# Where three operands of TensorE lie in the on-chip memory, modulo 512 bytes

## The chip, the cores and the metric

The kernel runs on one core of one Trainium2 chip. The metric is the device time of one execution in microseconds; the median of three runs of the kernel before is 2125.82 us (2125.45 to 2138.95).

## What is computed

Two stacks of transformer-like layers work on one sequence of 256 positions with 1024 channels, all in float32.

```
first stack, 2 layers:
  x -> hybrid_mixer (w_in 1024x7680; differential attention, neighbourhood attention, short
       convolution; gates; w_branch 3x512x1024; w_mix_out 1024x1024) -> layer_norm(alpha*x + h)
    -> memory_cross_attention (xa_q, xa_kv, xa_o) -> layer_norm(alpha*x + h)
    -> conv_ffn: (silu(dwconv(gt) + b) * u) @ w_out, with u, gt = split(x @ w_in), D_FF 2816
       -> layer_norm(alpha*x + h)
second stack, 2 layers:
  x + 0.5*swiglu(rms_norm(x))  ->  x + mix @ w_out  (pool, block attention, dilated attention,
  31-tap convolution; the four branches stand side by side in mix)  ->  x + 0.5*swiglu(rms_norm(x))
swiglu(x) = (silu(x @ wg) * (x @ wu)) @ wd, D_FF 2816
```

Nearly all the arithmetic lies in the products with weights.

## The kernel before, in words

**Weights.** All weight matrices are cut on the host into 336 chunks of 128 x 2048 floats (1 MB). SyncE fetches each into one of five slots of `raw`. ScalarE copies a chunk into one of four slots of `whi` with rounding to the reduced float32 format of TensorE (L782), and VectorE writes what is left, raw minus whi, into `wlo` (L1599). `wlo` and `raw` lie at the same addresses. In the same way each activation is kept in two parts: `xh` and `xl` for x, `fh` and `fl` for the gated product of the feed-forwards, `zh` and `zl` for the four branches of the second stack's mixer, `yh`/`yl`, `mh`/`ml`, `oh`/`ol` and `memh`/`meml` for the branches, the merged branches, the attention's output and the memory of the first stack.

**Products.** `product` (L1192) issues 48 matmuls of a chunk in a row, in 16 groups of three: the upper weights with the upper activation, the upper weights with the lower activation, the lower weights with the upper activation. Each has its own weight load of 128 x 128 floats and streams 256 columns; both operands come from the on-chip memory. All go through the helper `mm`, whose line is L1156, so this line stands for every matmul but the transposes (L1342, L1368, L1395). With kinds F, B and O the weight chunk is the stationary operand and the activation the moving one; with kind T it is the other way round (`va`, `vb`, `xv`, `up`, `vm`, `vd`).

**Order.** `plan` writes the order of all chunks out by hand: in each layer of the first stack the mixer (roles dq, dk, va, qb, kb, vb, gc, hc, gb, gate, branch, mo), the cross attention (xk, xv, xq, xo) and the feed-forward (fu, fg, fo; 33 chunks); in each layer of the second stack a feed-forward (sg, su, sd; 33 chunks), the mixer (cg to vd, then wo) and another feed-forward. Attention steps stand between the chunks as `steps`. TensorE takes everything in this order; at the end of a stage it waits for the norm of x.

**Addresses.** `sb` takes the tiles one behind the other, in the order of the program. A tile of n floats takes 4n bytes of each partition, rounded up to 32. The weights are first: `wlo` at byte 0 and `whi` at 40960, with slots of 8192 bytes and weight tiles of 512 bytes, so every weight tile begins at 0 modulo 512. Then comes `x` (8192 bytes), then `lead`, a tile that nothing uses: 48 floats, 192 bytes. So `xh`, `xl` and each of their 1024-byte rows begin at 192 modulo 512. `trail` (80 floats) fills up to 512 bytes. Further on, `lead_f` puts `fh` and `fl` at 192 modulo 512 and `lead_z` puts `zh` and `zl` at 320. `yh`, `yl`, `mh`, `ml`, `oh`, `ol`, `memh` and `meml` lie at 192 as well. Below, the **offset** of a matmul is the address of its moving operand minus that of its stationary operand, modulo 512.

| matmuls | chunks | offset before | offset after |
|---|---|---|---|
| kind F with xh, xl | dq, dk, qb, kb, gc, hc, gb, gate, xq, fu, fg, sg, su, cg, ca, qm, km, qd, kd | 192 | 128 |
| kind T with xh, xl | va, vb, up, vm, vd | 320 | 384 |
| fh, fl | fo, sd | 192 | 64 |
| zh, zl | wo | 320 | 224 |
| yh, mh, oh, memh as moving operands | branch, mo, xo, xk | 192 | 192 |
| memh, meml as stationary operands | xv | 320 | 320 |

Of the kernel before, what the change touches and what calls it, by code (L numbers as in the profile page):

```python
# [22 lines left out]
P = 128  # L23
# [215 lines left out]
def kernel_program(nc, xT, memT, consts, consts2, pos, par1, par2, bias, W, out):  # L239
# [3 lines left out]
    with ctx:  # L243
        def sb(name, shape, dt=F32, where=ctx):
            return where.enter_context(nc.sbuf_tensor(name, shape, dt))
# [8 lines left out]
        wlo = sb("wlo", [P, RAW_RING, CH], F32R)  # L254
        whi = sb("whi", [P, HI_RING, CH], F32R)
        x = sb("x", [P, KT, S])
        _lead = sb("lead", [P, 48])
        xh = sb("xh", [P, KT, S], F32R)
        xl = sb("xl", [P, KT, S], F32R)
        _trail = sb("trail", [P, 80])  # L260
        c0 = sb("c0", [P, NC0])
        ones = sb("ones", [P, P])
        par = sb("par", [P, NP1])
# [65 lines left out]
        ff = ExitStack()  # L329
# [12 lines left out]
        fa = sb("fa", [P, 512], where=ff)  # L342
        fth = sb("fth", [P, 512], where=ff)
        fp = sb("fp", [P, 512], where=ff)
        _lead_f = sb("lead_f", [P, 120], where=ff)
        fh = sb("fh", [P, 2, 2, S], F32R, ff)
        fl = sb("fl", [P, 2, 2, S], F32R, ff)
        posf = sb("posf", [P, S], where=ff)
        posi = sb("posi", [P, S], mybir.dt.int32, ff)
        hpad = sb("hpad", [P, 2, S + TAPS - 1], where=ff)  # L350
        sgm = sb("sgm", [P, 512], where=ff)
        yc = sb("yc", [P, 2, S], where=ff)
        yc2 = sb("yc2", [P, 2, S], where=ff)
        _lead_z = sb("lead_z", [P, 96], where=ff)
        zh = sb("zh", [P, KT, S], F32R, ff)
        zl = sb("zl", [P, KT, S], F32R, ff)
        ff.close()
# [2063 lines left out]
```

How the kernel before makes its waits and increments, by code:

```python
    def claim(self, pe, signal, key):  # L99
        if self.reader is not None:
            pe.wait_ge(self.reader[0].sem, self.reader[0].at(self.reader[1]))
        self.reader = (signal, key)
# [325 lines left out]
        def await_split(engine, c):  # L428
            engine.wait_ge(split_lo.sem, split_lo.at(c))
# [11 lines left out]
        def await_chunk(engine, c):  # L441
            signal, key = finished(c)
            engine.wait_ge(signal.sem, signal.at(key))
# [1 line left out]
        def await_x(engine, n, b):  # L445
            if n in ended:
                engine.wait_ge(resid.sem, resid.at((n, b)))
            elif n == 0:
                engine.wait_ge(x_in[b], 16)
            else:
                engine.wait_ge(xnew.sem, xnew.at((END1, b)))
# [213 lines left out]
        @block.sync  # L666
# [9 lines left out]
                    if old["kind"] == "M":  # L676
                        await_split(sp, old["c"])
                    else:
                        await_chunk(sp, old)
                src = memT if c["kind"] == "M" else W[c["p"]]
                sp.dma_start(raw[:, r, :], src).then_inc(landed[r], 16)
                for n in wins:
                    if c["c"] == by_role["dq", hs[n]["l"]][0]["c"] + 12 + hs[n]["j"]:
                        if nbias >= 3:
                            sp.wait_ge(biased.sem, biased.at(wins[nbias - 3]))
                        sp.dma_start(biasr[:, nbias % 3, :, :], bias[nbias]).then_inc(bias_in[nbias % 3], 16)
                        nbias += 1
            for b in range(NB):
```

## Time and profile before

| | |
|---|---|
| median of 3 runs | 2125.82 us (2125.45 to 2138.95) |
| the profiled execution's own time | 2125.48 us |
| its span, first to last instruction | 2123.7 us |
| TensorE: matmuls, weight loads | busy 2081.9 us (98%), 2030.7 us (96%), 17304 each |
| VectorE, ScalarE, GpSimd | 1436.2, 994.2, 78.8 us |
| data from HBM | 362.35 MB, 171 GB/s over the span |
| granted TensorE clock, mean | 0.993 |

The busy time of the matmuls is the union of overlapping instructions: a matmul's record is 276 to 292 ns long, while the next one begins some 115 ns after it. What a matmul costs is therefore read from the distance between starts, not from its duration. The rows that give this distance say how many matmuls a stretch of time holds.

### The profile page before, as it was taken

To read this page: it belongs to the slowest core of one execution; us is meant where nothing else is said; L and a number is where in the kernel's file an instruction comes from. 1 tells how busy PE (TensorE), PEld (TensorE's weight loads), DVE (VectorE), ACT (ScalarE), POOL (GpSimd) and SP (SyncE) were. 2 spreads that over 40 slices of the span, in tenths; PEclk is the share of its full clock that TensorE was granted. 3 is DMA by queue.
4 is the path that set the end of the run, shared out by engine and by line. 5 is a ranking of instruction groups with operands and counts; after the bars stand their busy time and mean duration, and the time that the engine had idled before them with its cause. 6 is when DMAs were issued, how large, how long until landed. Compare 5 with 4: busy or idle time off the path is not lost.

```text
span 2123.7 us, 39278 instructions
## 1 busy us (share of the span) xinstructions
PE 2081.9 (98%) x17304; PEld 2030.7 (96%) x17304; DVE 1436.2 (68%) x1690; ACT 994.2 (47%) x1166; POOL 78.8 (4%) x96
## 2 busy tenths in 40 slices
PE   7999999999999999998999999999999999999998
PEld 7999999999999999998999999989999999989997
DVE  6665574676776655747667775797666666897564
ACT  4554454444455544544444444455444444454442
POOL 1000010100010000101000100000000000000000
PEclk9999999999999999999999999999999999999999
DMA  5444554455544445534555355534555555434552
GB/s 211 154 164 161 193 187 150 152 192 198 199 163 154 164 162 195 184 130 161 192 180 178 142 199 194 183 120 144 196 198 193 185 194 189 176 117 159 199 191 87
DMA packets 52858, 365.94 MB, mean 172 GB/s; under 512 B 5904, under 2 KB 5904, under 8 KB 9296
## 3 DMA queue, kind: packets, MB, share of 16 engines
q1 hardware_dynamic: 52272, 361.21, 47.5%
q8 instruction: 137, 2.24, 0.4%
q0 software_dynamic: 416, 2.22, 0.3%
q14 instruction: 33, 0.27, 0.0%
HBM read 362.35 MB, written 1.05 MB: 171 GB/s over the span
## 4 chain that ended last, share of the span: by engine, by line
PE 87%; issue 9%; DVE 2%; POOL 1%; ACT 0%; DMA 0%; POOLq 0%; DVEq 0%; ACTq 0%
PE accM L1156 51%; PE scoreP L1156 18%; PE outP L1156 9%; PE turnP L1156 8%; PE turnP L1342 1%; DVE wlo L1599 1%; POOL x L727 1%; POOL small L713 0%; PE outP L1368 0%; PE turnP L1395 0%; ACT whi L782 0%; DMA x<-in_xT 0%; DVE xl L1739 0%; DVE diag L1774 0%; DVE small L1776 0%
## 5 line engine op out<-in xcount | busy, mean ns | idle before, releaser
L1599 DVE TENSOR_TENSOR wlo<-raw,whi 128x2048 fp32r<-128x2048 f32 x336 | 768.3, 2289 | 349.3 <-ACT whi L782 348.4
L782 ACT ACTIVATE whi<-raw 128x2048 fp32r<-128x2048 f32 x336 | 639.9, 1910 | 233.6 <-PE accM L1156 135.9
L1156 PE MATMUL accM<-xh,whi 128*128 128x256 f32 x1152 | 336.6, 292 | 5.5 <-DVE xl L1739 4.8
L1156 PE MATMUL scoreP<-xh,whi 128*128 128x256 f32 x1152 | 323.0, 280 | 7.9 <-DVE xl L1622 4.3
L1156 PE MATMUL accM<-xh,wlo 128*128 128x256 f32 x1152 | 322.9, 280 | 0.0
L1156 PE MATMUL accM<-xl,whi 128*128 128x256 f32 x1152 | 322.9, 280 | 0.0
L1156 PE MATMUL scoreP<-xl,whi 128*128 128x256 f32 x1152 | 321.1, 279 | 0.0
L1156 PE MATMUL scoreP<-xh,wlo 128*128 128x256 f32 x1152 | 321.0, 279 | 0.0
L1156 PE MATMUL accM<-fh,wlo 128*128 128x256 f32 x1056 | 292.5, 277 | 0.0
L1156 PE MATMUL accM<-fl,whi 128*128 128x256 f32 x1056 | 292.5, 277 | 0.0
L1156 PE MATMUL accM<-fh,whi 128*128 128x256 f32 x1056 | 292.5, 277 | 0.0
L1156 PEld LDWEIGHTS accM<-xh,whi 128*128 128x128 f32 x1152 | 218.1, 189 | 17.5 <-issue 16.1
L1156 PEld LDWEIGHTS scoreP<-xh,whi 128*128 128x128 f32 x1152 | 219.1, 190 | 8.8 <-issue 7.6
L1156 PEld LDWEIGHTS accM<-xl,whi 128*128 128x128 f32 x1152 | 217.9, 189 | 2.6 <-issue 2.4
L1156 PEld LDWEIGHTS accM<-xh,wlo 128*128 128x128 f32 x1152 | 219.6, 191 | 0.0
L1156 PEld LDWEIGHTS scoreP<-xl,whi 128*128 128x128 f32 x1152 | 218.3, 189 | 0.1
L1156 PEld LDWEIGHTS scoreP<-xh,wlo 128*128 128x128 f32 x1152 | 218.2, 189 | 0.0
L1156 PEld LDWEIGHTS accM<-fh,whi 128*128 128x128 f32 x1056 | 199.0, 188 | 0.0
L1156 PEld LDWEIGHTS accM<-fh,wlo 128*128 128x128 f32 x1056 | 198.3, 188 | 0.0
L1156 PEld LDWEIGHTS accM<-fl,whi 128*128 128x128 f32 x1056 | 198.2, 188 | 0.0
L1156 PE MATMUL turnP<-xh,whi 128*128 128x256 f32 x480 | 133.0, 277 | 0.0
L1156 PE MATMUL turnP<-xl,whi 128*128 128x256 f32 x480 | 133.0, 277 | 0.0
(283 smaller groups left out, 4164.1 us busy)
## 6 DMA issues: line engine op xcount, KB each, us to landing
raw<-in_W SPq DMA_DIRECT2D x336, 1024.0 KB, 4.8
biasr<-in_bias SPq DMA_DIRECT2D x16, 256.0 KB, 3.0
raw<-in_memT SPq DMA_DIRECT2D x2, 1024.0 KB, 4.9
cc<-in_consts POOLq DMA_DIRECT2D x1, 1408.0 KB, 6.8
x<-in_xT SPq DMA_DIRECT2D x4, 256.0 KB, 4.5
out<-x SPq DMA_DIRECT2D x4, 256.0 KB, 2.9
c<-in_consts SPq DMA_DIRECT2D x1, 464.5 KB, 6.3
par<-in_par POOLq DMA_DIRECT2D x2, 203.5 KB, 3.7
```

What stands on the lines that cost most here:

```text
L727: ins = nc.gpsimd.tensor_scalar(x[:, k, :], cen[:, b % 2, m * S:(m + 1) * S], g, bb, ALU.mult, ALU.add)
L782: nc.scalar.activation(whi[:, hi_slot(c), :], raw[:, raw_slot(c), :], ACT.Copy).then_inc(split_hi.sem, 1)
L1156: return nc.tensor.matmul(dst, a, b, start=start, stop=stop, skip_group_check=True)
L1342: ins = nc.tensor.transpose(turnP[:, k * S + t * P:k * S + (t + 1) * P], src[t][:, k * P:(k + 1) * P], ident)
L1599: v.tensor_tensor(wlo[:, raw_slot(c), :], raw[:, raw_slot(c), :], whi[:, hi_slot(c), :].bitcast(F32), ALU.subtract).then_inc(split_lo.sem, 1)
```

## The change

Only unused tiles change size or are added, so that three pairs of tiles lie elsewhere. No instruction, order, shape or wait changes.

```
-        _lead = sb("lead", [P, 48])
+        _lead = sb("lead", [P, 32])
         xh = sb("xh", [P, KT, S], F32R)
         xl = sb("xl", [P, KT, S], F32R)
-        _trail = sb("trail", [P, 80])
+        _trail = sb("trail", [P, 96])
...
-        _lead_f = sb("lead_f", [P, 120], where=ff)
+        _lead_f = sb("lead_f", [P, 88], where=ff)
         fh = sb("fh", [P, 2, 2, S], F32R, ff)
         fl = sb("fl", [P, 2, 2, S], F32R, ff)
+        _trail_f = sb("trail_f", [P, 32], where=ff)
...
-        _lead_z = sb("lead_z", [P, 96], where=ff)
+        _lead_z = sb("lead_z", [P, 72], where=ff)
         zh = sb("zh", [P, KT, S], F32R, ff)
         zl = sb("zl", [P, KT, S], F32R, ff)
```

`xh` and `xl` move down by 64 bytes, to 128 modulo 512; `fh` and `fl` by 128 bytes, to 64; `zh` and `zl` by 96 bytes, to 224. All other tiles stay where they are, since `trail` and `trail_f` make up for the smaller leads and nothing lies behind `zl`.

## Rows read from the trace of the kernel before

**Rows 1.** The page: busy time, share of the span and instructions of each engine.
```profile
PE 2081.9 (98%) x17304; PEld 2030.7 (96%) x17304; DVE 1436.2 (68%) x1690; ACT 994.2 (47%) x1166; POOL 78.8 (4%) x96
PEclk9999999999999999999999999999999999999999
```

**Rows 2.** The page: chain that ended last, share of the span by engine.
```profile
PE 87%; issue 9%; DVE 2%; POOL 1%; ACT 0%; DMA 0%; POOLq 0%; DVEq 0%; ACTq 0%
```

**Rows 3.** Windows of two like feed-forwards, L1156: busy (count), clock, DMA share, GB/s.
```profile
409.60:590.60 181.00, 180.38 (x1586) 179.90 (x1585) 1.00 0.54 193
969.80:1158.60 188.80, 188.77 (x1584) 188.80 (x1585) 0.99 0.53 187
```

**Rows 4.** The chain in order of time: start us, us, what; slow stretches.
```profile
182.63 105.27 PE accM L1156 x894
766.43 105.29 PE accM L1156 x894
1000.51 11.31 PE scoreP L1156 x96
1011.82 5.65 PE accM L1156 x48
```

**Rows 5.** The same view, fast stretches.
```profile
438.45 10.88 PE scoreP L1156 x96
498.29 5.44 PE accM L1156 x48
1204.01 10.88 PE scoreP L1156 x96
1802.87 10.88 PE scoreP L1156 x96
```

**Rows 6.** Windows, L1156: us, PE busy (count, with those in flight), clock, DMA.
```profile
1036.00:1156.00 120.00, 120.00 (x1021) 1.00 0.53 188
1230.00:1350.00 120.00, 120.00 (x1061) 1.00 0.55 193
1980.00:2100.00 120.00, 120.00 (x1061) 1.00 0.49 176
```

**Rows 7.** The chain again: chunks xv (offset 320) and xq (192).
```profile
304.92 5.44 PE accM L1156 x48
323.63 5.66 PE accM L1156 x48
```

**Rows 8.** Timeline, chunk wo (320): its third and its 48th matmul; start us, us.
```profile
1923.34 0.28 PE L1156 MATMUL accM<-zh,wlo 128*128 128x256 f32 x1
...
1928.64 0.28 PE L1156 MATMUL accM<-zh,wlo 128*128 128x256 f32 x1
```

**Rows 9.** Groups of matmuls by form: busy us, mean ns | idle before.
```profile
L1156 PE MATMUL accM<-va,eT 128*128 128x128 f32 x64 | 8.4, 274 | 0.0
L1342 PE MATMUL turnP<-c,ew 128*128 128x128 f32 x96 | 14.4, 272 | 0.0
L1156 PE MATMUL accM<-fh,whi 128*128 128x256 f32 x1056 | 292.5, 277 | 0.0
L1156 PE MATMUL scoreP<-kx,qx 128*128 128x256 f32 x64 | 15.1, 379 | 0.0
```

**Rows 10.** Timeline of TensorE: start us, us, instruction; eight matmuls of va and eT.
```profile
66.53 1.05 PE L1156 MATMUL accM<-va,eT 128*128 128x128 f32 x8
67.34 0.36 PE L1156 MATMUL accM<-xh,whi 128*128 128x256 f32 x1
```

**Rows 11.** Groups of VectorE and ScalarE that write at 192 and at 224.
```profile
L943 ACT ACTIVATE fh<-fp 128x512 fp32r<-128x512 f32 x66 | 41.8, 633 | 106.5 <-DVE fp L1866 64.8 <-DVE fp L1885 41.7
L924 ACT ACTIVATE fth<-fa 128x512 f32<-128x512 f32 x44 | 27.8, 633 | 181.7 <-DVE fa L1872 181.7
L2124 DVE SCALAR_TENSOR_TENSOR fl<-fp,fh 128x512 fp32r<-128x512 f32 x66 | 45.4, 688 | 20.0 <-ACT fh L943 20.0
L1878 DVE SCALAR_TENSOR_TENSOR fa<-fth,fa 128x512 f32<-128x512 f32 x44 | 30.1, 685 | 0.8 <-ACT fth L924 0.8
```

**Rows 12.** Idle time ahead of the split of the weights, by releaser.
```profile
L1599 DVE TENSOR_TENSOR wlo<-raw,whi 128x2048 fp32r<-128x2048 f32 x336 | 768.3, 2289 | 349.3 <-ACT whi L782 348.4
L782 ACT ACTIVATE whi<-raw 128x2048 fp32r<-128x2048 f32 x336 | 639.9, 1910 | 233.6 <-PE accM L1156 135.9
```

## The prediction

> **What bounds the kernel now.** The page comes first: matmuls are in flight for 98% of the span, the clock is at its upper level (2.4 GHz) throughout, and the engine behind, VectorE, is at 68% [rows 1]. The chain of waits says the same from its end: 87% of it is TensorE, the rest mostly short steps at the norms [rows 2]. The idle time of the two engines that split the weights is time in which they wait for TensorE or for each other, not time for which TensorE waits [rows 12]. So the time is the number of matmuls by the distance between their starts, and the next view has to be one that shows this distance.
>
> Two feed-forwards of the first stack show it. They do the same work on tiles at the same addresses, and one takes 181.0 us, the other 188.8 [rows 3]. The chain in order of time says where the 7.8 us lie: 96 matmuls take 11.31 us in the later one (117.8 ns each) and 10.88 in the earlier one (113.3) [rows 4, 5]. This is not a mean over good and bad matmuls. A window of 120 us holds 1021 or 1061 of them; with the 276 ns that a matmul stays in flight added to the window, that is 117.8 and 113.4 ns, the same as in the short stretches [rows 6]. So there are **two paces**, each held over more than a thousand matmuls, across chunks, slots, accumulators and both activations, until something interrupts the stream. The four feed-forwards of the second stack and the first of the first stack run at 113.3; the second of the first stack runs at 117.8, and so do the two stretches of gates, branches and mo, 894 matmuls in 105.3 us each [rows 4, 5]. Offset 192 shows both paces (rows 4 against rows 5, and xq [rows 7]); offset 320 does too: xv at 113.3 [rows 7], wo at 117.8 (45 distances in 5.30 us [rows 8]). The offset alone therefore does not choose the pace; how the stream of weights and the stream of columns come to lie against each other in time has a part in it.
>
> **The change, part by part.**
>
> *Tiles written elsewhere.* ScalarE and VectorE write and read xh, xl, fh, fl, zh and zl at other multiples of 32 bytes. Like operations that write at 192 and at 224 take 633 and 633 ns on ScalarE, 688 and 685 on VectorE [rows 11]. I take nothing. If it did cost 3 ns for each of some 500 such operations, that would be 1.5 us, and nearly all of it would be hidden by the stream of TensorE.
>
> *What stays.* branch (12 chunks), mo (8), xo (8), xk and xv (16) keep their offset, which leaves 336 - 44 = 292 chunks, or 14,016 matmuls, with a new one.
>
> *The slow pace in the moved chunks.* The difference of the two paces is (11.31 - 10.88) / 96 = 4.45 ns. At the slow pace are: the 33 chunks of the second feed-forward, 1584 matmuls, 7.0 us (the like stage says 7.8 with its start); the 16 gate chunks in the two long stretches, 768 matmuls, 3.4 us; and in the mixers and cross attentions of both stacks 59 chunks that run at it for half or more of their length (xq [rows 7] and wo [rows 8] are of this kind), with 2,318 distances of 116 to 121 ns by their starts, 10.3 us. Together 20.7 us.
>
> *The fast pace.* Whether 113.3 is a floor, no view shows, as no chunk runs faster. The nearest bound below: eight matmuls of va and eT, whose weight loads are of the same size and whose stream is half as long, take 1.05 us with a record of 274 ns for the last: (1.05 - 0.27) / 7 = 111 ns [rows 9, 10]. The far bound is the transposes, 14.4 us for 24 groups of four: (0.600 - 0.272) / 3 = 109 ns [rows 9]. Against them: those stream 128 columns, and the matmuls in question 256. Above, the nearest pace is the slow one, 117.8; the far bound is one more step of the same size, 122.2, an estimate that no row shows. I take 113.3, which both offsets share, for what a good offset gives, and keep 111 and 117.8 as the ends for the range.
>
> *What comes next if TensorE gets faster.* In a feed-forward VectorE and the transfers have room: 0.54 of the transfer engines' time [rows 3], 68% of VectorE [rows 1]. A gain of 3% would uncover neither, so a gain in pace is a gain in time.
>
> **The rivals.**
>
> *Forecast: the new offsets hold the fast pace.* The slow pace goes from the moved chunks and the fast one stays as it is: 2125.5 - 20.7 = 2104.8, say 2105 us; with half of the slow matmuls mended, 2115. For it: at 192 a slow feed-forward and a fast one differ by nothing but how they began, so 192 stands near a border, and another offset may stand further off. Chance 0.34.
>
> *A lower floor.* Both paces contain a loss that a better offset avoids. At 111 ns: 14,016 matmuls by 2.3 ns is 32 us, with the 20.7 together 53: 2072 us; at the far bound of 109, 60 + 21: 2045. For it: every matmul in question lasts 277 ns on record, while one of 256 columns that streams for longer (kx, qx) lasts 379 and va, eT 274, with half the columns [rows 9]; this fits a stream of weights that is in the way of the columns once in each matmul. Against: two offsets give exactly the same floor. Chance 0.25. The Trainium skill, "TensorE: Matmul & The Clock Gate", section "Wait — 56ns, not 53.3ns?", gives N / 2.4 + 2.5 ns for the distance of warm matmuls, which for 256 columns would be 109.2 and 57 us below the fast pace over the moved matmuls; no row here shows 256 columns at that distance.
>
> *The new offsets lock slow.* At 128 (most chunks) or 64 (fo, sd) the two streams meet in each matmul, the pace is 117.8 wherever an offset is new, and the five feed-forwards that are fast now lose most: 14,016 - 4,670 = 9,346 matmuls by 4.45 ns is 41.6 us: 2167 us. It decides in the feed-forwards: fo and sd alternate with sg, su, fu, fg, and as the pace is carried from chunk to chunk, one bad offset of the two may be enough for all. One step more would be 2125.5 + 41.6 + 62.4 = 2230. For it: the fast feed-forwards are good at 192 and have little to win and much to lose. From 25 us of loss on it outweighs all that the slow stretches can give back. Chance 0.22.
>
> *The pace is drawn, not set.* Which stage locks to which pace depends on the stages' starts and is drawn anew: a feed-forward is 7 us up or down, so 2118 to 2133 us. One of the three runs shown is 13 us above the others, which is two feed-forwards' worth. Chance 0.11.
>
> *Nothing.* The two streams do not meet in the memory at all and the paces have another cause: 2125.5 us. Against it stands that nothing in the rows tells the two feed-forwards apart but time. Chance 0.08. It is also a rule of the Trainium skill, "SBUF — State Buffer", section "SBUF: two separate sides": there, only the port that VectorE and GpSimd share causes contention, and TensorE never waits for anyone.
>
> **How the numbers follow.** The sum is made against the profiled execution's own 2125.48 us, 1.8 us more than its span and 0.3 below the median of the three runs, so it stands for the median too. The time is that of the forecast, 2105 us. About 1% (21 us) is what a measurement can tell from no change. Faster by more: the lower floor (0.25) and half of the forecast, which ends at that very border (0.17), 0.42. Within 1%: the other half (0.17), the drawn pace and nothing (0.19), 0.36. Slower by more: 0.22, as of the slow lock only ends below half its price fall within 1%. The range goes from 2065, which holds the floor at 111 ns with some room, to 2165, which holds nearly all of the slow lock; outside lie the far bounds on both sides, some 0.15. The forecast's own range is 2100 to 2117.
>
> **What would show it.** Right: the second feed-forward of the first stack takes 181 us, as the first does; 96 matmuls take 10.88 us in all feed-forwards; the stretches of gates hold pieces of 5.44 us among branches of 5.65 or less. A lower floor: 96 matmuls in 10.7 us or less, and records below 276 ns. Slow lock: 11.31 in the feed-forwards of the second stack. Drawn: one feed-forward changes its pace and the others stay. It would make the prediction wrong if the pace of a stage turned out to be set by how it begins, whatever the offset, or if the unmoved stages (branch, mo) changed as much as the moved ones.

## The result, and the profile after

The changed kernel takes 2171.16 us (median of four runs, 2169.8 to 2174.0), the kernel before 2132.39 us beside it (four runs, 2125.45 to 2140.71): a ratio of **1.0175 (1.0144 to 1.0207)**. It is slower, with the whole interval above 1, outside the predicted range of 2065 to 2165 us and against the forecast of 2105. The profiled execution took 2169.8 us with a span of 2168.0, which is 44.3 us longer than the profiled one of before.

The page of the changed kernel has nearly the same shares as [rows 1] and [rows 2], with longer busy times of TensorE (PE are its matmuls, PEld its weight loads):

```profile
PE 2126.7 (98%) x17304; PEld 2075.3 (96%) x17304; DVE 1440.4 (66%) x1690; ACT 993.6 (46%) x1166; POOL 78.5 (4%) x96
...
PE 87%; issue 9%; DVE 2%; POOL 1%; ACT 1%; DMA 1%; POOLq 0%; DVEq 0%; ACTq 0%
```

Both matmuls and weight loads are busy for 45 us more, the other engines for the same time as before within 5 us. The chain of waits in order of time shows where (start us, us, engine, tile, line and count; L1157 is L1156 of before, one line down):

```profile
440.72 11.38 PE scoreP L1157 x96
...
1010.98 11.39 PE scoreP L1157 x96
...
1153.09 16.96 PE accM L1157 x144
...
1216.04 11.39 PE scoreP L1157 x96
...
1803.31 11.39 PE scoreP L1157 x96
```

The pieces of 96 matmuls with xh and xl last 11.38 or 11.39 us in every feed-forward, 118.6 ns for one matmul, where [rows 5] has 10.88 and [rows 4] 11.31. The 144 of fo (1153.09) last 16.96, 117.8 ns. By their starts, none of the 292 moved chunks is faster than 117.7 ns, so the fast pace is gone from all new places, and the x chunks are even slower than the slow pace of before.

What stayed where it was went the other way. Windows of the line that issues the matmuls, in the first mixer: two branch chunks (offset 192), four gate chunks (now 128), four mo chunks (192):

```profile
201.90:212.50 10.60, 10.60 (x96) 1.00 0.53 198
224.20:246.80 22.60, 22.60 (x192) 1.00 0.51 187
263.40:284.80 21.40, 21.40 (x191) 1.00 0.61 203
```

With 276 to 281 ns for those in flight these are 113.3, 119.2 and 113.5 ns (118.7 for the gates by the starts within the chunks). In the kernel before all three kinds were at 117.8 [rows 4]: branch and mo, whose offset did not change, became faster and the gates slower.

The whole difference, by the distances between starts within the chunks in the two traces, longer interruptions (over 400 ns) left out: kind F with xh and xl +35.2 us (1111.7 to 1147.0), fo and sd +11.6 (353.8 to 365.5), kind T +0.6, wo +0.3, branch -2.4, mo -1.7; the rest is 0.1 or less each. That is 43.6 of the 44.3 us; with every interruption counted in, it is 42.3.

### The profile page after: what moved, and what is told of

Same layout as the page of the kernel before. It is cut to its first block, busy times and chain, and to the rows that moved or that the text cites. A ratio compares the mean times of both kernels' runs of the same rounds, so it can differ in the third digit from the quotient of the medians.

```text
span 2168.0 us, 39278 instructions
## 1 busy us (share of the span) xinstructions
PE 2126.7 (98%) x17304; PEld 2075.3 (96%) x17304; DVE 1440.4 (66%) x1690; ACT 993.6 (46%) x1166; POOL 78.5 (4%) x96
## 4 chain that ended last, share of the span: by engine, by line
PE 87%; issue 9%; DVE 2%; POOL 1%; ACT 1%; DMA 1%; POOLq 0%; DVEq 0%; ACTq 0%
PE accM L1157 51%; PE scoreP L1157 18%; PE outP L1157 9%; PE turnP L1157 8%; PE turnP L1343 1%; POOL x L728 1%; DVE wlo L1600 1%; DMA raw<-in_W 0%; ACT whi L783 0%; PE outP L1369 0%; PE turnP L1396 0%; POOL small L714 0%; DMA x<-in_xT 0%; DVE xl L1740 0%; DVE x L1657 0%
## 5 line engine op out<-in xcount | busy, mean ns | idle before, releaser
L1157 PE MATMUL accM<-xh,whi 128*128 128x256 f32 x1152 | 338.8, 294 | 5.3 <-DVE xl L1740 4.8
L1157 PE MATMUL scoreP<-xh,whi 128*128 128x256 f32 x1152 | 327.5, 284 | 7.8 <-DVE xl L1623 4.3
L1157 PE MATMUL scoreP<-xh,wlo 128*128 128x256 f32 x1152 | 326.0, 283 | 0.0
L1157 PE MATMUL scoreP<-xl,whi 128*128 128x256 f32 x1152 | 325.9, 283 | 0.0
L1157 PE MATMUL accM<-xh,wlo 128*128 128x256 f32 x1152 | 325.4, 282 | 0.0
L1157 PE MATMUL accM<-xl,whi 128*128 128x256 f32 x1152 | 325.2, 282 | 0.0
L1157 PE MATMUL accM<-fh,whi 128*128 128x256 f32 x1056 | 295.8, 280 | 0.0
L1157 PE MATMUL accM<-fh,wlo 128*128 128x256 f32 x1056 | 294.7, 279 | 0.0
L1157 PE MATMUL accM<-fl,whi 128*128 128x256 f32 x1056 | 294.7, 279 | 0.0
L1157 PEld LDWEIGHTS accM<-xh,whi 128*128 128x128 f32 x1152 | 218.2, 189 | 17.2 <-issue 16.1
L1157 PEld LDWEIGHTS scoreP<-xh,whi 128*128 128x128 f32 x1152 | 218.7, 190 | 8.8 <-issue 7.6
L1157 PEld LDWEIGHTS accM<-xl,whi 128*128 128x128 f32 x1152 | 218.3, 189 | 2.6 <-issue 2.4
L1157 PEld LDWEIGHTS scoreP<-xl,whi 128*128 128x128 f32 x1152 | 218.7, 190 | 0.1
L1157 PEld LDWEIGHTS scoreP<-xh,wlo 128*128 128x128 f32 x1152 | 218.7, 190 | 0.0
L1157 PEld LDWEIGHTS accM<-xh,wlo 128*128 128x128 f32 x1152 | 218.0, 189 | 0.0
L1157 PEld LDWEIGHTS accM<-fh,wlo 128*128 128x128 f32 x1056 | 198.5, 188 | 0.0
L1157 PEld LDWEIGHTS accM<-fh,whi 128*128 128x128 f32 x1056 | 198.2, 188 | 0.0
L1157 PEld LDWEIGHTS accM<-fl,whi 128*128 128x128 f32 x1056 | 197.6, 187 | 0.0
L1157 PE MATMUL outP<-xh,wlo 128*128 128x256 f32 x480 | 135.3, 282 | 0.0
L1157 PE MATMUL turnP<-xh,whi 128*128 128x256 f32 x480 | 135.3, 282 | 0.0
```

The source lines that it names most:

```text
L1157: return nc.tensor.matmul(dst, a, b, start=start, stop=stop, skip_group_check=True)
```

## The experiments

All are the kernel before with other unused tiles; what is computed is the same in each. Pace means the mean distance between starts of neighbouring matmuls of a kind, interruptions above 130 ns left out. "x chunks" are those of kind F with xh and xl.

**e1, x alone at 128.**

```
-        _lead = sb("lead", [P, 48])
+        _lead = sb("lead", [P, 32])
-        _trail = sb("trail", [P, 80])
+        _trail = sb("trail", [P, 96])
```

> Only xh and xl move (offset 128); fh, fl stay at 192 and zh, zl at 320. Theory A, the offset itself sets the pace of a matmul: all chunks with xh and xl run at 118.6 ns between starts as in the changed kernel, fo and sd between them at 113.3 (as the branch chunks, unmoved at 192, do there right behind gates at 118.6); about 9,500 matmuls that lose 5.3 or 0.9 ns give some 35 us, less some 6 us that branch, mo, fo and sd of the slow stages win back: 2150 to 2158 us. Rival B, the pace is carried from chunk to chunk: fo and sd run at 117.8 or more behind the slow chunks though their own offset is 192, and the time is that of the changed kernel, 2166 to 2171 us. Rival C, it was drawn at the start of each stage: stages differ among themselves as they do in the kernel before.

Measured: 2158.24 us, ratio 1.0163 (1.0126 to 1.0201). x chunks at 118.7 ns in all stages; fo and sd at 113.6 in five feed-forwards and 116.6 in the sixth. The chain in a feed-forward of the second stack, then in the second of the first stack, sd and fo being the accM pieces:

```profile
1213.46 11.40 PE scoreP L1156 x96
1224.85 5.45 PE accM L1156 x48
...
1003.61 5.65 PE accM L1156 x48
1009.26 11.39 PE scoreP L1156 x96
...
1151.37 16.32 PE accM L1156 x144
```

A chunk at 192 is fast (5.45 us) directly behind chunks at 118.7: the slow pace is not handed on. This holds for five stages. In the sixth, eight chunks of fo have 5.65 us and its last three are fast (16.32 us for 144 matmuls), so 192 has two paces again and changes between them within one stage. The time lies 0.2 us above the upper end of theory A's; B is ruled out.

**e2, the gated product alone at 64.**

```
-        _lead_f = sb("lead_f", [P, 120], where=ff)
+        _lead_f = sb("lead_f", [P, 88], where=ff)
+        _trail_f = sb("trail_f", [P, 32], where=ff)
```

> Only fh and fl move (offset 64); xh, xl stay at 192 and zh, zl at 320. Theory A: fo and sd run at 117.8 everywhere, 2,585 of their matmuls lose 4.45 ns, 11.5 us; the x chunks keep 113.3 where they have it: about 2137 us. Rival B, carried: the first fo or sd of a stage pushes the x chunks behind it to 117.8 too, and as 192 holds both paces they stay there; five feed-forwards by 7 us each, 35 us: about 2160 us. Rival D, 64 costs only beside x at 128: no change, 2125 to 2133 us.

Measured: 2148.16 us (2140.63 to 2150.74), 1.0111 (1.0074 to 1.0147): between A and B, and neither's number. fo and sd run at 117.8 in all six feed-forwards, as A has it. The x chunks run at 113.4 in two feed-forwards and at 117.7 in the other four. The chain in two stages, the second feed-forward of the first stack and the first of the second:

```profile
996.52 5.66 PE accM L1157 x48
1002.18 11.31 PE scoreP L1157 x96
...
1233.67 5.65 PE accM L1157 x48
1239.32 10.89 PE scoreP L1157 x96
```

In the second stage sd chunks of 117.8 ns at 64 and x chunks of 113.4 ns at 192 alternate; in the first the x chunks stay at 117.7. So 64 costs by itself, and with it around, 192 holds its slow pace in more stages of this execution; why is not shown. D is ruled out.

**e3, the mixers' branches alone at 224** (`lead_z` 96 to 72).

> Only zh and zl move (offset 224): 384 matmuls of wo. Theory A: by the changed kernel's wo chunks (118.4 ns against 117.8) the cost is below 1 us; the time is that of the kernel before within its own scatter of runs (2125 to 2141 us). Rival B: the chunk ahead of a feed-forward decides how it locks, and one or more of the feed-forwards behind the mixers changes its pace by 7 us.

Measured: 2126.45 us, 0.9994 (0.9967 to 1.0022); wo at 118.3 ns. As expected, nothing that shows in the time. In the profiled run one feed-forward behind a mixer was at 117.8 and the second of the first stack at 113.3, the reverse of [rows 3], at the same total. Rival B had named just such a change; but as the kernel before changes by the same steps from run to run (below), this one trace cannot tell whether the chunk ahead caused it.

**e4, the two offsets change places**: x at 64 (`lead` 16, `trail` 112), fh at 128 (`lead_f` 104, `trail_f` 16).

> The two offsets change places: xh, xl at 64, fh, fl at 128, zh, zl at 320. Theory A, only the offset counts and not the tile: x chunks run at 117.8 and fo, sd at 118.6; against the changed kernel the 9,500 x matmuls of kind F win 0.8 ns (8 us) and 3,100 lose 0.8 (2.5 us): about 2164 us. Rival E, the tile counts (its neighbours, its row order in the stream): x chunks stay at 118.6 and fo, sd at 117.8 whatever the offset.

Measured: 2164.72 us, 1.0194 (1.0163 to 1.0226); x chunks 117.6, fo and sd 118.6. The chain (accM pieces are sd):

```profile
1215.43 11.31 PE scoreP L1157 x96
1226.74 5.70 PE accM L1157 x48
```

The paces changed places with the offsets, and theory A's time was right within 1 us. The tile has no part in it.

**h1, the weights move and the activations don't.**

```
+        _first = sb("first", [P, 16])
         landing = ExitStack()
-        _lead = sb("lead", [P, 48])
+        _lead = sb("lead", [P, 32])
```

> An unused tile of 64 bytes goes ahead of the weights, and the lead ahead of xh shrinks by 64 bytes, so only the weights (and x, which TensorE reads at the norms alone) move: weights at 64 modulo 512, and xh, fh, yh, mh, oh, memh at the addresses of the kernel before. Every offset from 192 becomes 128, zh's becomes 256. Theory A, the distance to the weights counts: x, fo, sd, branch, mo at 118.6, wo at 120; 9,439 matmuls by 5.3 ns and 5,930 by 0.9: about 2180 us. Rival H, the activation's own address counts: the two paces of before, 2118 to 2139 us.

Measured: 2181.28 us, 1.0246 (1.0176 to 1.0316). x chunks, fo, sd, branch, mo and xk all at 118.7, wo (256) at 119.8. The stretch of gates, branches and mo, slow but uniform:

```profile
189.91 100.18 PE accM L1157 x843
```

100.18 / 843 = 118.8 ns, where branch and mo stood at their old addresses. This is the plainest of the runs: **the distance between the two operands counts, not where the activation lies.** The new distances also have the paces that other runs found for them by moving the activation: 128 has 118.7 (e1), 256 has 119.8 for wo and 119.9 for the x chunks of g1, and xv, at 384, has 118.8 where kind T of the changed kernel has 118.5. Only one new place of the weights was tried.

**g1 to g4, other offsets.** Only numbers of the leads and trails differ from the edits above, and g2 has no `lead_z` (g1: x 256, fh 0, zh 64; g2: 448, 320, 448; g3: 320, 448, 0; g4: 160, 352, 192).

> xh, xl at 256, fh, fl at 0, zh, zl at 64. Theory F, what counts is the offset modulo 128, with 64 the good residue and 0 the bad one (so far 128 and 384 gave 118.6, 224 gave 118.3, and 64, 192, 320, 448 between 113.3 and 117.8): x chunks and fo, sd at 118.6, about 2168 us. Rival G, it is the place modulo 512 in a matmul where the two streams meet: 0, where they would meet at its very beginning, differs clearly from 128 in one direction or the other (113 or below, or above 120), and 256 differs from 128 too.

> xh, xl at 448, fh, fl at 320, zh, zl at 448. Theory F: both have the good residue 64 modulo 128, so both paces, 113.3 and 117.8, are open: 2118 to 2160 us, stages drawn one by one. Rival G: 448 is its own case; T chunks at 448 ran at 115.0 in the run with xh at 64, so x chunks of kind F may hold 115 or the fast 113.3 throughout, which gives 2120 us or less; fo and sd at 320 take 113.3 or 117.8 as wo and xv do.

> xh, xl at 320, fh, fl at 448, zh, zl at 0. Theory F: as the run before, both paces open, drawn stage by stage. Rival G: 320 is the mirror of 192 and behaves as the kernel before (2118 to 2140 us); fo and sd at 448 show the pace of 448 beside chunks at 320.

> xh, xl at 160, fh, fl at 352, zh, zl at 192: half steps, both 32 modulo 128 or 96 modulo 128 (160 = 128 + 32, 352 = 256 + 96). Theory F: by the one case so far (224, residue 96, 118.3) both lie between the good and the bad residue, near the bad: 118 to 118.6, about 2165 us. Rival G: distance from 192 or 320 alone counts, and 32 bytes off the good places give a pace between 113.3 and 118.6, one and steady.

Measured: g1 2190.21 us, 1.0282 (1.0232 to 1.0332); g2 2139.41, 1.0038 (1.0017 to 1.0060); g3 2155.87, 1.0123 (1.0087 to 1.0159); g4 2171.17, 1.0192 (1.0143 to 1.0242). The chain in a feed-forward, of g1, g2, g3 and g4 in turn:

```profile
1018.29 11.52 PE scoreP L1157 x96
1029.81 5.76 PE accM L1157 x48
```
```profile
1496.20 10.89 PE scoreP L1156 x96
1507.09 5.65 PE accM L1156 x48
```
```profile
1503.26 11.30 PE scoreP L1157 x96
1514.56 5.45 PE accM L1157 x48
```
```profile
1513.23 11.27 PE scoreP L1157 x96
1524.50 5.75 PE accM L1157 x48
```

In these pieces g1 has 120.0 ns for both, g2 113.4 for x at 448 and 117.7 for sd at 320, g3 117.7 for x at 320 and 113.5 for sd at 448, g4 117.4 for x at 160 and 119.8 for sd at 352. Theory F (period 128) fell with g1, which it put at 118.6 and 2168 us; and it gave 320 a fast pace that no fo or sd and hardly an x chunk had. Rival G was wrong too where it made 320 the mirror of 192. For g4 both had too fast a pace: F's time was 2165 us, and fo and sd at 352 lie above the 118.6 at which G's band ends. The fast pace does occur at 320, in three x chunks in a row of g3's first feed-forward, of which the middle one is

```profile
424.30 5.44 PE turnP L1157 x48
```

and in one chunk wo each of e2 and e4; at 64, three of e4's 204 x chunks have it. What fits is a period of **256**: 0 and 256 at 120.0, 128 and 384 at 118.6, 64 and 320 at 117.8 with single chunks at 113.3, 192 and 448 at either 113.3 or 117.8 for whole stages.

**h2 to h4, steps of 8 and 16 bytes about 192.** The two parts of x, and of fh, are cut from one tile with a few floats ahead of them; as in h2 for x:

```
-        xh = sb("xh", [P, KT, S], F32R)
-        xl = sb("xl", [P, KT, S], F32R)
+        xhl = sb("xhl", [P, 6 + 2 * KT * S], F32R)
+        xh = xhl[:, 6:6 + KT * S].rearrange("p (k s) -> p k s", k=KT)
+        xl = xhl[:, 6 + KT * S:6 + 2 * KT * S].rearrange("p (k s) -> p k s", k=KT)
```

> Steps of 8 bytes about the good place: xh, xl at 184, fh, fl at 200. Theory J, 192 is the edge of a plateau (64 bytes further down, 128, has only a slow pace; 32 up, 224, has 118.3): one of the two sides holds 113.3 throughout, without the 117.8 that 192 also holds, the other is slow. If it is this side for x: all feed-forwards at 113.3 for sg, su, fu, fg, and 2105 to 2118 us. Theory K, 192 is a single point because operands are read in blocks of 64 bytes: both 184 and 200 have one pace of 117 to 119, about 2165 us.

> The mirror: xh, xl at 200, fh, fl at 184. Theory J: if the run before is the slow side, this is the fast one, 2105 to 2118 us, and the other way round. Theory K: about 2165 us as well.

> Steps of 16 bytes: xh, xl at 176, fh, fl at 208. Theory J: 176 lies between 160 (117.7) and 184, 208 between 200 and 224 (118.3), and the good side shows how wide the plateau is. Theory K: 117.7 for 176 and 118.3 for 208, as at 160 and 224: 2160 to 2166 us.

Measured: h2 2189.90 us, 1.0285 (1.0231 to 1.0339); h3 2192.82, 1.0301 (1.0255 to 1.0346); h4 2177.03, 1.0226 (1.0156 to 1.0296). Paces: x at 184 120.0, at 200 120.3, at 176 119.2; fo and sd at 200 120.4, at 184 119.9, at 208 117.7 (a mixture of 117 and 119 by chunk). The chain of h2 in a feed-forward, sd at 200 and then an x chunk at 184:

```profile
1237.23 5.79 PE accM L1158 x48
1243.01 5.76 PE turnP L1158 x48
```

There is no plateau: 8 bytes on either side of 192 lie paces as bad as that of 0. Theory J fell, and K, which was right in that both sides are slow, had them too fast by 1 to 3 ns (2165 us against 2190); for h4 it had 2160 to 2166 us against 2177. One rival is untested: 184 and 200 are multiples of 8 bytes and not of 32, while the weights stayed at a multiple of 512. No run moved both by 8 bytes, so it is not shown whether the distance or the finer alignment of the activation's own address costs here.

**i1 and i2, x chunks and fo, sd at the two good offsets in turn** (i1: `lead_f` 56, `trail_f` 64; i2: `lead` 112, `trail` 16, `lead_z` taken out).

> xh, xl at 192, fh, fl at 448, zh, zl at 320. Theory L, at a change of offset the pace is drawn anew, and 448 behind 192 falls into the fast one (fo, sd at 448 ran at 113.5 in five of six feed-forwards though the x chunks at 320 between them ran at 117.8): all six feed-forwards near 113.3, and 2118 us in every run, without the steps of 7 us between runs. Rival M, within a feed-forward the pace is carried across equal-quality offsets as it is with 192 alone: whole feed-forwards at 113.3 or 117.8, runs of 2118, 2125, 2132, 2139 us as before.

> The mirror: xh, xl and zh, zl at 448, fh, fl at 192. Theory L: fast from the first fo or sd of each feed-forward on, about 2118 us. Rival M: whole feed-forwards at either pace, 2118 to 2139 us. If 448 itself is worse for the x chunks than 192 (they had 115.5 on average there, with fo and sd at 320), 2125 to 2140 us with mixed chunks.

Measured: i1 2122.60 us, 0.9996 (0.9977 to 1.0015); i2 2119.86, 0.9998 (0.9978 to 1.0019). Both profiled runs had all six feed-forwards at 113.3 to 113.5. A piece of i1 and one of i2:

```profile
1515.44 10.88 PE scoreP L1157 x96
1526.32 5.44 PE accM L1157 x48
```
```profile
1517.13 10.88 PE scoreP L1155 x96
1528.01 5.44 PE accM L1155 x48
```

But their other runs had the old steps: i1's ten lie between 2118.3 and 2120.6 or between 2124.6 and 2127.3, i2's between 2117.3 and 2120.3 or at 2125.4 and 2125.5, with one at 2133.1. That is rival M. Offset 448 is as good as 192, and mixing them doesn't remove the slow pace. No version beats the kernel before by a measurable amount.

## Why the prediction was wrong, point by point

**What bounds the kernel** was right: the time is the number of matmuls by the distance between their starts. Distances between starts explain 43.6 of 44.3 us, and no other engine is needed for it. Two readings were slightly off and change nothing: the two rows give (11.31 - 10.88) / 96 = 4.48 ns, where the prediction writes the 4.45 of the unrounded starts, and the clock was not at its upper level throughout, but at its lower one for 7 us at the beginning of two feed-forwards (below).

**The fast pace: this is the step that failed.** "I take 113.3, which both offsets share, for what a good offset gives" made 113.3 the property of any offset, and the slow pace an accident that another offset would leave behind ("another offset may stand further off"). The runs show the reverse: 113.3 for whole stages belongs to 192 and 448 alone. At 64 and 320 it is rare (the chunks named above, and xv [rows 7], where the roles are turned round), and no chunk at any other offset tried came below 116.6. So in place of the 20.7 us that the moved chunks were to win, they lost 47.7: x chunks went to 118.7 ns, fo and sd to 117.8, wo to 118.3.

| offset | pace, ns | from |
|---|---|---|
| 0, 256 | 120.0, 119.9 | fo, sd; x chunks of g1 |
| 64 | 117.8, 117.8, 117.6 (rarely 113.3) | fo, sd after and in e2; x chunks of e4 |
| 128 | 118.7, 118.7, 118.6, 118.7 | x chunks after and in e1; fo, sd of e4; all of h1 |
| 160, 176, 184 | 117.7 (chunks of 117.3 and of 118.7), 119.2, 120.0 | x chunks of g4, h4, h2 |
| 192 | 113.3 or 117.8 | before, i1, i2; branch and mo |
| 200, 208, 224 | 120.3, 117.7, 118.3 | h3; h4; wo in e3 |
| 320, 352 | 117.8 (rarely 113.3), 119.8 | fo, sd of g2, g4 (x chunks of g3 at 320: 117.6) |
| 448 | 113.3 or 117.8 | i1, i2, g2, g3 |

What the trace of before held, and the prediction used too lightly: wo at offset 320 was at the slow pace in 45 distances in a row [rows 8], and kind T with xh and xl was slow for the most part (117.5 ns on average). "Two offsets give exactly the same floor" leant on one chunk of xv (two of its eight are fast).

**The slow pace in the moved chunks**, 20.7 us to win, was a sum of the right size for chunks at 192 that happen to be slow; the change left them at a slow pace and took the 113.3 from the others.

**The rival "the new offsets lock slow" is what happened**, and its price was nearly right: 41.6 us against 44.3. Its parts were off in three ways, and that the total is so close is partly luck: x at 128 is at 118.7 and not 117.8, so that the moved chunks lost 47.7 us, 6 more than priced; branch and mo won 4.1 us back; and its reason, that one bad offset makes the other slow, is wrong in five of six feed-forwards of e1. For x at 192 beside 64 (e2) it is left open, with four of six slow. The chance of 0.22 was too low. The range ended at 2165 although this rival's own number was 2167: a bound cut 2 us below the case that it was to take in.

**"The pace is drawn"** holds, but for whole stages at 192 and 448 only. The 56 runs of the kernel before in all comparisons lie in four groups with nothing between them: 16 at 2117.7 to 2121.0, 21 at 2124.2 to 2127.7, 15 at 2131.7 to 2134.9 and 4 at 2139.0 to 2140.7, in steps of the 7 us that one feed-forward's pace is worth (33 chunks by 48 by 4.45 ns). Profiled executions fit this: 2125.5 us with one slow feed-forward (before; 2125.9 in e3), 2118.3 and 2119.8 with none (i1, i2). The four runs of the changed kernel, which has no fast pace to draw in its feed-forwards, lie within 4.2 us. So the kernel before is slower than its best by a step or more in 40 of 56 runs, and a ratio against it depends on the draw: its median was between 2124.5 and 2132.4 us in the five comparisons.

**"Nothing"**, the case of the Trainium skill, "SBUF — State Buffer", section "SBUF: two separate sides" (TensorE never waits for anyone), was wrong in its time: addresses alone moved it, and h1, which moved the weights by 64 bytes, was 2.5% slower. That rule is about one engine and another, though, and no run here shows TensorE waiting for another engine's access; whether its own two reads disturb each other is the open point below. The distance of 109.2 ns for 256 columns, an estimate from the formula in the Trainium skill, "TensorE: Matmul & The Clock Gate", section "Wait — 56ns, not 53.3ns?", was not held by any chunk of any run; the best is 113.3.

**Writes at other multiples of 32 bytes** cost nothing that could be seen: ScalarE and VectorE are busy as before within 0.6 and 4.2 us, and the writes of fl take 688 ns on average, as before [rows 11].

**What stays open.** That TensorE reads its two operands at once and that these two reads get into each other's way at certain distances fits all of it, but no run shows the reads themselves; it is argued. Nor is it shown what decides between the two paces at 192. In the first mixer branch and mo were fast behind gates at 128, 256 and 184 (after, e1, g1, h2) and slow behind gates at 192, 64, 160, 200, 176, 320 and 448 (before, e2, e3, e4, g4, h3, h4, g3, g2, i1, i2), the same in both mixers of a trace; in the feed-forwards it changes from run to run. One rival can be put aside, that a drop of the granted clock ahead of a stage makes it slow. The stretch in which the second feed-forward of the first stack begins (at 969.8 us), in the trace of before and in that of e3; the granted clock is the number behind the busy times:

```profile
968.00:974.00 6.00, 4.17 (x19) 4.20 (x20) 4.54 (x8) 4.26 (x8) 5.74 (x9) 0.50 0.02 3
```
```profile
968.00:974.00 6.00, 4.08 (x19) 4.11 (x20) 4.57 (x7) 4.26 (x9) 5.73 (x9) 0.50 0.01 3
```

The clock is at its lower level, 1.2 GHz, in both (0.50), and this feed-forward ran at 117.8 ns in the first trace and at 113.3 in the second. The slow feed-forward of e3 has no such drop ahead of it.

## What to carry to other kernels

When a stream of short matmuls with a weight load each is the bound, measure the distance between starts by stage, not the busy time, and look whether it has steps: equal stages at different paces point to how the two operands lie against each other. Treat the distance between them in bytes as a parameter to be scanned on the chip, in steps of 8 bytes rather than 32 or 64; a good place can be a single point with bad ones beside it, and a tile inserted ahead of one operand and not of the other moves it. Measure more than once: a good place can still hold two paces. And when a case has a price, the range must hold that price.

## What the runs showed of the hardware that was not expected

The pace of matmuls of 128 x 128 by 256 in float32's reduced format, at the granted 2.4 GHz, runs from 113.3 to 120.4 ns averaged over the chunks of a kind in a trace, with nothing of the arithmetic changed; that is 6%; over all runs the kernels took 2117.3 to 2194.2 us, 3.6%. Places 256 bytes apart behave alike (0 and 256, 64 and 320, 192 and 448), and with the activation moved by 8 bytes from 192 the pace goes from 113.3 to 120. With h2 to h4 the way in which the tiles are declared changed as well. The records of the weight loads do not tell these places apart. The same group in g1 (x at 256), in the changed kernel (128) and in e2 (192); the number behind the comma is the mean in ns:

```profile
L1157 PEld LDWEIGHTS scoreP<-xh,wlo 128*128 128x128 f32 x1152 | 223.1, 194 | 0.0
```
```profile
L1157 PEld LDWEIGHTS scoreP<-xh,wlo 128*128 128x128 f32 x1152 | 218.7, 190 | 0.0
```
```profile
L1157 PEld LDWEIGHTS scoreP<-xh,wlo 128*128 128x128 f32 x1152 | 220.9, 192 | 0.0
```

By these lines e2's weight loads are longer than the changed kernel's, while the same group in the kernel before, also at 192, has 189; the total share of the weight loads is 96% in every kernel. The distance between starts has it the other way round: 118.7 ns in the changed kernel, and 116.3 on average over the x chunks of e2.
